# Five state space steps ahead of the attention, with the compressed keys' products between them

## What is computed

```python
z = rmsnorm_2(h, norm_mix[i]) @ w_in[i]
q, kc, vc, ksl, vsl, kw, vw, g, u = jnp.split(z, split_at, axis=-1)
...
o_nsa = nsa_attention(q, kc, vc, ksl, vsl, kw, vw, gates, ...)
o_s5 = s5_mixer(u, ...)
h = h + jnp.concatenate([o_nsa, o_s5], axis=-1) @ w_out[i]

def compress(kv, pe, w1, w2):          # 31 windows of 32 tokens
    ...
    return jax.nn.gelu(blk @ w1) @ w2

def s5_mixer(u, ...):                   # a linear recurrence over the tokens
    bu = lax.complex(bu_re, bu_im) * b_coef
    _, state = lax.associative_scan(combine, (a_seq, bu), axis=1)
    y = real(state) @ c_re - imag(state) @ c_im + d_skip * u
    ...
```

## Time and profile before

| | us |
| --- | --- |
| median of 3 runs | 3353.84 |
| lowest and highest | 3346.92, 3365.6 |
| the profiled execution's own time | 3353.96 |
| its span, first to last instruction | 3352.2 |
| PE busy (share) | 2973.5 (89%) |
| DVE busy | 1120.3 (33%) |
| ACT busy | 740.0 (22%) |
| POOL busy | 460.2 (14%) |

### The profile page before, as it was taken

One profiled execution on the slowest core, in us unless ns is written; L12 is line 12 of the kernel. 1 busy time (PEld: TensorE's weight loads), 2 busy tenths in 40 slices (PEclk: granted clock), 3 DMA queues, 4 the chain that ended last, 5 costly groups with the idle time before them and its releaser, 6 DMA issues.

```text
span 3352.2 us, 36468 instructions
## 1 busy us (share of the span) xinstructions
PE 2973.5 (89%) x15448; PEld 2039.8 (61%) x15448; DVE 1120.3 (33%) x2211; ACT 740.0 (22%) x1337; POOL 460.2 (14%) x463
## 2 busy tenths in 40 slices
PE   5989798989968899889998968999997678999997
PEld 3777655454457565465454546888646555588876
DVE  3973210000055333310000014323273983432234
ACT  4142110111031143111111113212101333221223
POOL 0000132222210043023323210000000221000000
PEclk8999799999979999889999988999997789999998
DMA  6612799999841231279999961333111002132321
GB/s 241 200 42 115 285 383 399 402 398 396 334 139 52 88 126 51 116 267 401 409 407 403 408 239 51 103 99 101 57 64 73 1 1 101 51 101 91 98 77 56
DMA packets 131881, 622.02 MB, mean 186 GB/s; under 512 B 14063, under 2 KB 85871, under 8 KB 97408
## 3 DMA queue, kind: packets, MB, share of 16 engines
q0 software_dynamic: 40160, 403.75, 29.9%
q1 hardware_dynamic: 90400, 210.87, 18.0%
q10 hardware_dynamic: 1152, 4.98, 0.4%
HBM read 613.25 MB, written 29.36 MB: 192 GB/s over the span
## 4 chain that ended last, share of the span: by engine, by line
PE 60%; DMA 16%; DVE 8%; issue 2%; ACT 1%; POOL 1%; SPq 0%; DVEq 0%; POOLq 0%; ACTq 0%
PE ps L92 58%; DMA ring<-in_exp_up,wix 14%; DVE scr L106 3%; PE ps L95 2%; DVE scr L126 1%; DMA hrows<-scr 1%; DVE scr L120 1%; DVE hT L114 1%; DVE hT_r L106 1%; DVE scr L114 0%; POOL ring L135 0%; DVE hT L129 0%; ACT hT L98 0%; DVE xT L114 0%; DMA scr<-yrows 0%
## 5 line engine op out<-in xcount | busy, mean ns | idle before, releaser
L92 PE MATMUL ps<-ring,scr 128*64 128x512 f32 (+3 forms) x3136 | 734.9, 563 | 67.4 <-DMA ring<-in_exp_up,wix 66.2
L92 PE MATMUL ps<-ring_r 128*128 128x512 f32 (+1 forms) x2544 | 752.7, 377 | 40.2 <-DVE hT_r L106 31.3
L92 PEld LDWEIGHTS ps<-ring_r 128*128 128x128 f32 x2544 | 469.7, 191 | 154.5 <-issue 37.5
L92 PEld LDWEIGHTS ps<-ring,scr 128*64 128x64 f32 (+2 forms) x3136 | 290.1, 154 | 425.5 <-issue 417.9
L92 PE MATMUL ps<-scr,ring 128*128 128x128 f32 (+4 forms) x3744 | 435.5, 306 | 42.1 <-DMA ring<-yrows 20.7
L92 PE MATMUL ps<-hT_r,ring_r 128*128 128x512 f32 (+1 forms) x1224 | 461.0, 377 | 0.0
L92 PEld LDWEIGHTS ps<-scr,ring 128*128 128x128 f32 (+2 forms) x3744 | 396.6, 194 | 83.5 <-issue 71.7
L106 DVE TENSOR_TENSOR scr<-scr,ps 64x512 f32<-64x512 f32 (+1 forms) x72 | 49.7, 690 | 782.5 <-ACT scr L98 439.3
L92 PE MATMUL ps<-scr_r,ring_r 128*128 128x512 f32 x1104 | 259.6, 396 | 0.6 <-DVE scr_r L106 0.6
L92 PEld LDWEIGHTS ps<-hT_r,ring_r 128*128 128x128 f32 x1224 | 234.3, 191 | 40.1 <-issue 2.0
L92 PE MATMUL ps<-ring 128*128 128x512 f32 (+10 forms) x712 | 186.4, 521 | 69.0 <-DVE scr L114 54.7
(11 more groups left out here) (140 smaller groups left out, 2466.2 us busy)
## 6 DMA issues: line engine op xcount, KB each, us to landing
ring<-in_ffn_w SPq DMA_DIRECT2D x66, 1024.0 KB, 5.5
ring<-in_mod_w SPq DMA_DIRECT2D x12, 2048.0 KB, 7.9
ring<-in_mod_w SPq DMA_DIRECT2D x16, 1024.0 KB, 5.0
scr<-in_mod_w SPq DMA_DIRECT2D x8, 1024.0 KB, 7.5
ring<-in_exp_gate SPq DMA_DIRECT2D x4, 2048.0 KB, 13.1
ring<-in_exp_up SPq DMA_DIRECT2D x4, 2048.0 KB, 15.7
ring<-in_exp_down SPq DMA_DIRECT2D x4, 2048.0 KB, 20.8
ring<-in_w_in SPq DMA_DIRECT2D x4, 2048.0 KB, 8.1
```

What stands on the lines that cost most here:

```text
L92: return self.real.matmul(o, l, r, start=start, stop=stop) if self.real else Quiet()
```

## The change

The number of state space steps ahead of the attention becomes five (`AHEAD`). In the stretch ahead of it TensorE goes through five rounds: a piece of other work (two tiles of the 280 column projection in the first round, one half of a compressed product in each of the four others), then the inputs of state space step i + 1, then the outputs of step i. `compressed` now does one half at a time. In the attention loop state space step n + 5 is done in step n, for n up to 10; steps 11 to 13 have none.

The first weights of the compressed keys no longer go through slot 4. They go to places of their own, `Mx.cw`: the columns 512 to 767 of each of hT's eight pieces, which the mixer's normalized input leaves free, and the ring columns of the four buffers `Mx.PT`. SyncE issues the two transfers after the first two projection weights, once the feed-forward stage of ScalarE, VectorE and TensorE is over. The values' weights follow the 280 column weights in slot 4.

```diff
-    wr = Slots([signal(f"slot{i}_landed") for i in (0, 1, 2, 3, 4, 5, "2_half0", "2_half1", "_piece0", "_piece1")], ps)
+    wr = Slots([signal(f"slot{i}_landed") for i in (0, 1, 2, 3, 4, 5, "2_half0", "2_half1", "_piece0", "_piece1", "_windows")], ps)
...
+    Mx.cw = [hT[:, :].rearrange("p (k t) -> p k t", k=8)[:, :, 512:768],
+             ring[:, r_[0] - 3072:r_[0] - 1024].rearrange("p (k n) -> p k n", k=8)]
+
+    AHEAD = 5
+
...
-                (("cmp", 0), I["cmp_w1"][0], 16, 256), (("cmp", 1), I["cmp_w1"][1], 16, 256)]):
-            weights_load(e, 5 if i % 2 and i < 6 else 4, ("mix", *name), src, nk, n)
+                (("cmp", 1), I["cmp_w1"][1], 16, 256)]):
+            weights_load(e, 5 if i % 2 else 4, ("mix", *name), src, nk, n)
+            if i == 1:
+
+                for x in (act_stage, dve_stage, pe_stage):
+                    e.wait_ge(*x.of("ffn1_"))
+                wr.take(10, "mix", "cmp", 0)
+                for h in range(2):
+                    e.dma(Mx.cw[h], I["cmp_w1"][0][:, 8 * h:8 * h + 8, :]).then_inc(
+                        *wr.load("mix", "cmp", 0))
...
-        def rest():
+        def rest(*tiles):
             e.wait_ge(*wr.there("mix", "v"))
-            for i in range(4):
+            for i in tiles:
...
-        def compressed(br):
+        def compressed(br, m):
             e.wait_ge(*dve_step.of("windows", br))
             e.wait_ge(*wr.there("mix", "cmp", br))
-            for m in range(2):
-                o = ps.take("cmp", br, m)
-                e.wait_ge(*ps.ready("cmp", br, m))
-                for p in range(16):
-                    c = 62 * (16 * br + p)
-                    x = e.matmul(o[:, 0:62], weights(("mix", "cmp", br), 256, p, 128 * m, 128 * m + 128), Mx.kp[:, c:c + 62],
-                                 p == 0, p == 15)
-                x.then_inc(*ps.fill("cmp", br, m))
-            wr.done(("mix", "cmp", br), "cmp", br, 1)
+            o = ps.take("cmp", br, m)
+            e.wait_ge(*ps.ready("cmp", br, m))
+            for p in range(16):
+                c = 62 * (16 * br + p)
+                w = (weights(("mix", "cmp", 1), 256, p, 128 * m, 128 * m + 128) if br else
+                     Mx.cw[p // 8][:, p % 8, 128 * m:128 * m + 128])
+                x = e.matmul(o[:, 0:62], w, Mx.kp[:, c:c + 62], p == 0, p == 15)
+            x.then_inc(*ps.fill("cmp", br, m))
+
...
+        rest(0, 1)
         s5_inputs(0)
-        for br in range(2):
-            compressed(br)
+        for i in range(AHEAD):
+            if i == 0:
+                rest(2, 3)
+                wr.done(("mix", "v"), "mx_v", 3)
+            else:
+                compressed(*divmod(i - 1, 2))
             for half in range(2):
-                ps.release("s5_in", br, half)
-            s5_inputs(br + 1)
-            s5_output(br)
-        ps.release("s5_y", 0)
+                ps.release("s5_in", i, half)
+            s5_inputs(i + 1)
+            s5_output(i)
+            if i:
+                ps.release("s5_y", i - 1)
...
         for n in range(18):
             if n < 16:
                 scores(n)
-            if 1 <= n < 15:
-                s5_output(n + 1)
+            at = n + AHEAD
+            if n and at <= 16:
+                s5_output(at - 1)
             if n >= 2:
                 values(n - 2)
-            if n < 14:
+            if at < 16:
                 for half in range(2):
-                    ps.release("s5_in", n + 2, half)
-                if n < 13:
-                    s5_inputs(n + 3)
-            if n < 15:
-                ps.release("s5_y", n + 1)
+                    ps.release("s5_in", at, half)
+                if at < 15:
+                    s5_inputs(at + 1)
+            if at <= 16:
+                ps.release("s5_y", at - 1)
...
-        s5(0)
-        s5(1)
+        for n in range(AHEAD):
+            s5(n)
         e.wait_ge(*ps.filled("vcm", 1))
         for n in range(17):
             if n < 16:
                 scores(n)
             if n >= 1:
                 normal(n - 1)
-            if n < 14:
-                s5(n + 2)
-            if n == 14:
+            if n + AHEAD < 16:
+                s5(n + AHEAD)
+            if n + AHEAD == 16:
                 s5_output(15)
```

More of the change, by code:

```diff
@@ L2401, in rest @@
                 x.then_inc(*ps.fill("mx_v", i))
-            wr.done(("mix", "v"), "mx_v", 3)
         for wi, m, dst, late, j in projections():
@@ L2414, in pe_mixer2 @@
                 turn_late(late)
-        rest()
-        def compressed(br):
+        def compressed(br, m):
             e.wait_ge(*dve_step.of("windows", br))
             e.wait_ge(*wr.there("mix", "cmp", br))
-            for m in range(2):
-                o = ps.take("cmp", br, m)
-                e.wait_ge(*ps.ready("cmp", br, m))
-                for p in range(16):
-                    c = 62 * (16 * br + p)
-                    x = e.matmul(o[:, 0:62], weights(("mix", "cmp", br), 256, p, 128 * m, 128 * m + 128), Mx.kp[:, c:c + 62],
-                                 p == 0, p == 15)
-                x.then_inc(*ps.fill("cmp", br, m))
-            wr.done(("mix", "cmp", br), "cmp", br, 1)
+            o = ps.take("cmp", br, m)
[6 more added lines that the diff above has]
+            x.then_inc(*ps.fill("cmp", br, m))
         def s5_inputs(n):
@@ L2455, in s5_output @@
             x.then_inc(*ps.fill("s5_y", n))
+        rest(0, 1)
         s5_inputs(0)
-        for br in range(2):
-            compressed(br)
-            for half in range(2):
-                ps.release("s5_in", br, half)
-            s5_inputs(br + 1)
-            s5_output(br)
-        ps.release("s5_y", 0)
+        for i in range(AHEAD):
[4 more added lines that the diff above has]
+                compressed(*divmod(i - 1, 2))
+            for half in range(2):
+                ps.release("s5_in", i, half)
[3 more added lines that the diff above has]
+                ps.release("s5_y", i - 1)
+        wr.done(("mix", "cmp", 0), "cmp", 0, 1)
+        wr.done(("mix", "cmp", 1), "cmp", 1, 1)
         o = ps.take("kcm")
```

## The result

The changed kernel takes 3337.27 us (median of 9 runs, 3334.25 to 3344.02); the kernel before, run beside it, 3353.84 (9 runs). The ratio is 0.995, 95% interval 0.9937 to 0.9963: 16.6 us faster. The forecast was 3336.0. The profiled execution took 3337.44, its span 3335.5, 16.7 less than the span before.

The account below looks back on a forecast made before the run. TensorE and the weight queue were taken to bound the stretch before the attention, VectorE the attention loop. Gains of 3 + 0.7 + 13.9, plus something under 1, made 18 us: 3353.96 to 3336, range 3327 to 3346.

Parts of the forecast that it names:

- Before the attention: Stretch up to the first score: five state space steps fit, most products at the lower clock; gain 3 us.
- 3.6 us: Before the attention: TensorE waits this long for VectorE's state space step 1, with the lower clock taken from there on.
- my own signs: Wrong if the period before the attention is not near 10.8, its clock is high, or steps 11 to 13 exceed 30 us.
- The rival of the full clock: Before the attention: clock stays at its upper level, VectorE sets the pace; gain 6.4 there, 21 in all, 3333; chance 0.15.
- Steps 0 to 10: Attention loop: three steps shorter by 0.6 without carry, two longer by 0.56 for the carry's add; net gain 0.7 us.
- Waits on line 114: Attention steps 0 to 10: TensorE's waits for VectorE's last state space instruction stay, 10 or 11 in place of 14.
- Steps 11 to 13: Attention loop: without VectorE's state space work they take 26.5 us in place of 40.4; gain 13.9.
- something under 1 for a TensorE that idles less: Last attention steps: a further small gain, added to 17.6 to make 18 us.
- The rival of the last steps hanging on ScalarE: Steps 11 to 13 run as one chain like step 15, low clock before the attention; gain 11, 3343; chance 0.22.
- cost nothing: Before the attention: the early transfers of the first compressed weights delay no needed work; cost zero.
- Theory A: Whole change: the gain is VectorE's work moved from the loop to where VectorE is idle; the load is only a condition.
- theory B: Before the attention: the early load carries the gain, removing two waits and the clock loss behind; deeper lead adds little or costs.

Follow-up runs that it names:

- with the waits filled: The changed kernel plus four extra products of 512 columns, results overwritten, ahead of the outputs of state space steps 1 to 4; 3337.22 us, ratio 0.9956.
- three ahead: The changed kernel with three state space steps ahead in place of five, weights still early; 3331.66 us, ratio 0.9937; with extra overwritten products 3334.93 us, ratio 0.9936.
- the load alone: The changed kernel with only the early weights kept, two steps ahead and rounds as before; 3328.42 us, ratio 0.9924; a second time 3321.13 us, ratio 0.9904.
- the tail filled: The changed kernel plus two extra products of 512 columns, results overwritten, in each of attention steps 12 to 14; 3332.67 us, ratio 0.9947.
- the lead alone: The changed kernel, five ahead, with the keys' first weights loaded through slot 4 again as in the kernel before; 3351.17 us, ratio 0.9992.

## Why the prediction was right, and what it had wrong

**The total.** 3336.0 forecast, 3337.3 measured; 18 us of gain forecast, 16.6 measured. In front of the attention and in steps 0 to 13 the mechanism was as described; in the last steps it was not, and the parts came out with these sizes.

**Before the attention**, gain 3 forecast, 3.2 measured. The layout came out: first half at the upper clock, one wait "3.6 us" (3.48), the lower clock behind it, no wait on compressed weights, the first score 63.2 us behind S where 63.6 was forecast. Part of this is luck, for three errors cancelled. The end of that wait comes 1.6 us later than laid out, most of it since VectorE's step 0 took 1.4 us longer, below. The work behind it took 29.5 us and not 34.4, since the clock came back for one round (0.93 in the window from 2567). And so there is one more wait, 2.96 us. By my own signs this was partly wrong: VectorE's steps began 10.1 us apart in the mean, not 10.8, and the clock was not near 0.50 all the way. The rival of the full clock priced this stretch at a gain of 6.4; with the waits filled it was 4.4 (66.4 - 62.0).

With three ahead, products of 62 columns ran 13.6 us on end at 0.50, as 13.90 us of them did before, though the same products hold 1.00 where they begin with it (7.40 us in the kernel with the load alone). The clock rose again in the inputs and outputs behind them or soon after. The Trainium skill (TensorE: Matmul & The Clock Gate, the HAM clock gate) has sustained work bring the full clock; the trace disagrees for these 13.6 us.

**Steps 0 to 10**, 0.7 forecast, 2.3 measured. The carry's adds cost 0.5 and 0.3 and the missing carries gave 2.2 (0.55, 0.85, 0.76), as costed within 0.4; step 6, 0.9 shorter, has no term in my sum and is scatter: the ten profiles show it at 13.8 or at 14.5 to 14.7, with either lead. Over four profiles each, steps 0 to 10 take 149.2 us two ahead and 148.0 five ahead, so 1.1 is the better figure. Waits on line 114: 11, as forecast.

**Steps 11 to 13**, 13.9 forecast, 14.2 measured: 8.7, 7.8 and 9.7 us where I had some 10, 7 and 9.

**The last steps** are where a term has the wrong sign: "something under 1 for a TensorE that idles less" came out as a loss of 3.2. The window of before, beside that of after from 2764.2:

```profile
2781.10:2816.30 35.20, 28.56 (x192) 22.80 (x192) 7.15 (x44) 18.98 (x53) 9.91 (x18) 0.85 0.37 150
```

TensorE idles no less: 6.6 us before, 6.5 after (length less its busy time), most of it in waits of up to 2.7 and 2.0 us for ScalarE and GpSimd. Its work takes 3.4 us longer, at a mean clock of 0.73 in place of 0.85. That was a clock cost, as the 31.7 us at 1.00 with the tail filled show; I had costed only the waits. It repeats: 38.1 and 39.1 us in two other kernels five ahead, 33.4 and 35.8 with the load alone. What lowered the clock there is not shown. The rival of the last steps hanging on ScalarE had this in it but put it in steps 11 to 13.

**The step that failed, beside this term, is the reading behind the sum.** I wrote that "the change takes three state space steps out of this loop and puts them in the stretch where VectorE is idle" and had the loads "cost nothing", which is so, but gave the waits that they remove no worth of their own. VectorE was idle there because TensorE waited for the compressed weights, 12.7 us, and then worked at half clock, another 16.5. Once the early load removes both, the idle stretch does not exist, and three steps in it cost 25.3 us to save 11.4. The two parts of the change are substitutes for the larger part: each fills or removes the same hole. The sum held, apart from the luck told above, since both ends of it were laid out instruction by instruction with both parts in; it says what the change does, and nothing on what each part does. Theory A falls as the account of the whole, though its price for the loop was right; theory B stands.

**Open:** why F to G with three ahead (223.9 and 224.3) is no shorter than with two (223.1 and 224.8) although step 13 loses its state space work (9.3 and 10.7 us in place of 12.2 and 11.7); the profiles show 38.1 and 37.4 us from step 14 on in place of 33.4 and 35.8. The granted clock there is 0.78 and 0.82 against 0.90 and 0.81, so it can be a part of it at most; not tested apart.

## What to carry to other kernels

A wait of TensorE can cost twice: its own time, and the clock of what follows; here 12.0 us of waits had 16.5 us of slower products behind them. Where another engine sets the pace the second part is worth little (1.2 us five ahead). Before work is moved into an engine's idle stretch, ask what makes it idle, and whether the same change takes that away; a lead pays only as deep as the other engine's own work covers it. And run each part alone: a total that comes out as forecast can still hide a part that costs.

## What the runs showed of the hardware

**A wait and the clock behind it.** Where TensorE stood 0.70 or 1.62 us its products went on at 1.00; behind 1.94, 2.96, 3.48 and 7.57 us they ran at 0.50. The length of the single wait does not decide it: in the attention loop products went on at 1.00 behind waits of 2.25, 2.31 and 2.63 us (kernel after) and behind this one of 2.17 us (load alone):

```profile
2756.19 0.48 PE L92 MATMUL ps<-ring 31*128 31x128 f32 x2 [2.17 <-ACT ring L102]
```

So a wait is not known to be harmless or costly until the clock behind it has been read.

**VectorE beside GpSimd.** Two VectorE products of 512 columns that read and write `scr` took 1.29 us before and with the load alone, and 2.66 after (2539.22 above), for the state space step begins one round earlier there, while GpSimd forms its tables. GpSimd's timeline of the kernel after:

```profile
2537.62 1.09 POOL L106 TENSOR_TENSOR ring<-ring 128x512 f32<-128x512 f32 x1
2538.80 1.05 POOL L106 TENSOR_TENSOR ring<-ring,scr 128x512 f32<-128x512 f32 x1
2539.92 1.42 POOL L106 TENSOR_TENSOR ring<-ring 128x512 f32<-128x512 f32 x1
```

With the load alone GpSimd had ended by 2530, ahead of VectorE's first product. The five other kernels that begin this step a round earlier show 2.55 to 2.99 us, the lead alone among them, so it does not come from the early load. The Trainium skill (GPSIMD Engine Reference, Specifications) names this contention, for VectorE instructions with two inputs in SBUF; the trace agrees, with 1.4 us on the path, though no run took GpSimd's work away to show it.
